# A hybrid attention layer: the cross-attention scores in two PSUM banks of their own, directly behind the stick-breaking scores

## The chip, the cores and the metric

The kernel runs on one core of one Trainium2 chip. The metric is the device time of one execution in microseconds (us). Three runs of the kernel before took 1628.17, 1628.67 and 1628.81 us, so the median is 1628.67 us. A separate execution was profiled; all rows below are from that one.

## The reference, cut to what matters

One layer over 4096 tokens of width 1024. RMSNorm(x) goes through one input projection of width 3072, whose parts feed three branches; each branch is multiplied by silu of its gate, and the three side by side go through an output projection that is added to x.

```
h = rmsnorm(x, norm_g)
sb_q, sb_k, sb_v, sb_gate, lru_x, lru_gate, xa_q, xa_gate = split(h @ w_in)
# stick-breaking attention: 8 heads of 64, q and k normed, strictly causal
z = q @ k.T / 8 ; log_fail = where(s < t, -softplus(z), 0)
w = where(s < t, exp(log_sigmoid(z) + sum of log_fail over the later keys), 0) ; sb = w @ v
# recurrent branch: causal convolution of 4 taps, two gates, a linear scan over time
h_t = a_t * h_(t-1) + u_t
# cross-attention: 4 heads of 64, q and k normed, 256 memory tokens
xa = softmax(xq @ mk.T / 8) @ mv
out = x + concat(sb * silu(sb_gate), lru * silu(lru_gate), xa * silu(xa_gate)) @ w_out
```

## The kernel before, in words

The tokens are worked on in NT = 32 tiles of 128. All weights stay in SBUF as pairs of float16 halves (high and low), and a product is three matmuls per 128 input columns: high by high, high by low, low by high (`pair_product`, L1479 to L1481). `project(c, ...)` is one 512-wide chunk of the input projection, 24 matmuls of 128x512; there are six per tile, in the order q, k, cross-attention q with its gate, recurrent input with its gate, stick-breaking gate, v. They alternate between PSUM banks 0 and 1. The output projection is two more such products (`out_first`, `out_second`).

The order is written out by hand: each engine runs `body(n, p)` for n from -1 to 33 (most of them in a loop over pairs of steps), and semaphores tie the engines together. `have(engine, signal, tile)` makes the engine wait until `signal` has been raised for `tile`. In step n the input projection is that of tile n, the scores and the rest of the attention are those of tile n-1, the output projection is that of tile n-2, and x of tile n+1 is prepared. Each engine and each DMA queue takes its instructions strictly in order.

PSUM has eight banks of 512 float32 columns. Banks 0 and 1 are `PROJ`, 2 and 3 `SCORE` (one for the even heads, one for the odd), 4 and 5 `TURN`, 6 `SMALL`, 7 `HEADS`. In the steady loop nothing uses `TURN`; only the set-up in steps -1 and 0 does (`memory_turn`, `memory_keys_turn`), and a tail that is entered only where the attention has to look further back than the neighbouring keys (`row`).

TensorE's step n, in its order:
- `project(0)` (q).
- `near_scores(1)`: two transposes (L1510) for the convolution, then 48 small matmuls of 64x64 by 128 columns (L1523), the stick-breaking scores of tile n-1, into `SCORE`. They wait until the exponentials of tile n-2 have read `SCORE` (`p_done`).
- `project(1)` (k), `project(2)` (cross-attention q and gate).
- the cross-attention scores of tile n-1: 12 matmuls of 64 rows by 256 columns (L1598), also into `SCORE`. They wait for `sig`, the sigmoids that have read the stick-breaking scores out of it.
- eight float32 matmuls for the recurrent gates (L1609), `project(3)`, `project(4)`, the 48 matmuls that multiply the stick-breaking weights with v (L1641), `project(5)`.
- `spread_rows` (L1620): two matmuls that spread the row scales of tile n+1 over the partitions. They wait for the diagonal that VectorE makes (`x_diag`, L1189).
- `out_first`, `out_second`, `values_product` (L1559 to L1564).

ScalarE's step n: `project(0)`'s result out of PSUM and its squares, the four sigmoids over `SCORE` (L711, L712, raising `sig`), after `project(1)` the keys out of PSUM (L752) and their squares (L754), after `project(2)` xq and its gate (L768 to L771), then the stick-breaking weights to float16 (L719), the recurrent gates (L787 to L794), the four exponentials of the cross-attention over `SCORE` (L801), the squares of x of tile n+1 (L809), the recurrent input and its gate (L814, L815), the float16 halves of q, k and xq (L822), a square root (L832), the gate sigmoid of `project(4)` (L836), the exponentials to float16 (L845), v (L857), x to float16 (L864). Four of these need another table (ACT_TABLE_LOAD).

VectorE's step n: the convolution, the sums of q's squares, those of k's squares (L1140), the stick scan (L1150) and the weights (L1156), the sums for xq, the low halves (L1168), the maximum of the cross-attention scores over `SCORE` (L1229), the norms (L1241), steps for the recurrent gates, the gates' products (L1201), the low halves of q, k, xq (L1261), the recurrent scan (L1276), the diagonal of the row scales (L1189), and what follows for x and the output.

SyncE issues the DMAs. Ahead of the transposing DMAs of q, k and xq of tile n it waits for `xa_scores`, since the xq buffer is read by L1598. At n = 31 (`last_one`) a second `near_scores(0)` follows the last projections but one, and waits for those DMAs.

Of the kernel before, what the change touches and what calls it, by code (L numbers as in the profile page):

```python
# [32 lines left out]
ACT = mybir.ActivationFunctionType  # L33
# [16 lines left out]
def hybrid_layer(nc, x, x_turned, mem, w_in_g, w_out_g, w_kv_v, per_partition, gain_rows, gate_blocks, out):  # L50
# [4 lines left out]
    HD = 64  # L55
    HS = D // 2 // HD
    HX = D // 4 // HD
    NM = mem.shape[1]
# [27 lines left out]
    with ctx:  # L86
# [24 lines left out]
        probs = fail_g[:, at:at + HX * NM].rearrange("p (h m) -> p h m", m=NM)  # L111
# [18 lines left out]
        xq_t = sb("xq_t", [P, 2, HX // 2, P], F16)  # L130
# [3 lines left out]
        mk_t = sb("mk_t", [P, 2, HX // 2, NM], F16)  # L134
# [65 lines left out]
        mx = few(HX)  # L200
# [31 lines left out]
        SCORE = bank[2:4]  # L232
        TURN = bank[4:6]
# [11 lines left out]
        s = {n: sem("t_" + n) for n in names}  # L245
# [3 lines left out]
        qk_turned = sem("qk_turned")  # L249
# [52 lines left out]
        def have(eng, signal, tile, each=1, short=0, ahead_of_loop=False):  # L302


            if not isinstance(tile, int) or tile >= 0:
                eng.wait_ge(signal, each * (tile + 1) - short)
                if ahead_of_loop or (not isinstance(tile, int) and eng.engine.name in alone):
                    eng.sem_inc(passed, 1)
# [332 lines left out]
        def _(act):  # L641
# [58 lines left out]
            def body(n, p):  # L700
# [3 lines left out]
                last_one, after, end = near_end(n)  # L704
# [22 lines left out]
                if B and not after:  # L727
                    have(act, qk_turned, n - 1, 96)
                    for part in range(2):
                        last = act.activation(k_t[:, p, part, :, 0:HALF], k_t[:, q, part, :, P:], ACT.Copy)  # L730
# [47 lines left out]
                if B:  # L778

                    have(act, s["gates_done"], n - 1)  # L780
                    have(act, s["h_done"], n - 2)
                    if isinstance(n, int) and n == 1:
                        act.wait_ge(mv_made, 2)
                    for g, (dst, bias) in enumerate(((rec_g, brg), (in_g, big))):
                        for h in range(LH):
                            at = (g * LH + h) * P
                            last = act.activation(dst[:, h, :], SMALL[:, at:at + P], ACT.Sigmoid, bias=bias[:, h:h + 1])  # L787
                    last.then_inc(s["gates_read"], 1)
                    have(act, s["gates_read"], n - 1)
                    if isinstance(n, int) and n == 1:  # L790
                        act.wait_ge(lam_made, 2)
                    for h in range(LH):
                        act.activation(tanh_l[:, h, :], rec_g[:, h, :], ACT.Tanh, scale=rate[:, h:h + 1])
                        last = act.activation(decay[:, h, :], rec_g[:, h, :], ACT.Exp, scale=rate[:, h:h + 1])  # L794
                    last.then_inc(s["tanh_done"], 1)

                    have(act, s["neg_done"], n - 1)
                    have(act, s["rden_done"], n - 2)
                    have(act, s["p_low"], n - 2)
                    for h in range(HX):  # L800
                        last = act.activation(probs[:, h, :], SCORE[h % 2][:, (h // 2) * NM:(h // 2 + 1) * NM], ACT.Exp,  # L801
                                              bias=neg_mx[:, h:h + 1], scale=near_scale[:, 1:2], accum_out=den[:, h:h + 1])
                    last.then_inc(s["p_done"], 1)
                if X:
# [6 lines left out]
                if A:  # L811
# [8 lines left out]
                    for raw, half in zip((q_raw, k_raw, xq_raw), halves_of_heads(n, 0)):  # L820
                        scale = QTOP if raw is not k_raw else gain_inv[:, 0:1]
                        last = act.activation(half, raw[:, :, :].rearrange("p h d -> p (h d)"), ACT.Copy, scale=scale)  # L822
# [82 lines left out]
        def _(dve):  # L905
# [180 lines left out]
            def body(n, p):  # L1086
# [22 lines left out]
                last_one, after, end = near_end(n)  # L1109
# [116 lines left out]
                if B:  # L1226
                    have(dve, s["xa_scores"], n - 1)
                    for odd in range(2):
                        last = dve.tensor_reduce(mx[:, odd::2], SCORE[odd][:, :].rearrange("p (h s) -> p h s", s=NM),  # L1229
                                                 AX.X, ALU.max)  # L1230
                    last.then_inc(s["mx_done"], 1)
                    have(dve, s["mx_done"], n - 1)
                    dve.tensor_scalar(neg_mx[:, :], mx[:, :], past_scale[:, 1:2], None, ALU.mult).then_inc(s["neg_done"], 1)
# [3 lines left out]
                if A:  # L1237
                    have(dve, s["rs_done"], n)
                    have(dve, s["k_gained"], n)
                    for raw, at, heads in ((q_raw, 0, HS), (k_raw, HS, HS), (xq_raw, 2 * HS, HX)):  # L1240
                        last = dve.tensor_tensor(raw[:, :, :], raw[:, :, :],  # L1241
                                                 rs[:, at:at + heads].unsqueeze(2).to_broadcast([P, heads, HD]), ALU.mult)
# [13 lines left out]
                if A:  # L1256
                    silu(s["lru_read"], s["gate_l"], PROJ[1][:, LW:GC], slice(D // 2, D // 2 + LW), G_LRU)
                    have(dve, s["qk_high"], n)
                    for raw, high, low in zip((q_raw, k_raw, xq_raw), halves_of_heads(n, 0), halves_of_heads(n, 1)):
                        scale = QTOP if raw is not k_raw else gain_inv[:, 0:1]  # L1260
                        last = dve.scalar_tensor_tensor(low, raw[:, :, :].rearrange("p h d -> p (h d)"), scale, high,  # L1261
                                                        ALU.mult, ALU.subtract)
# [10 lines left out]
                if B:  # L1273
                    have(dve, s["u_done"], n - 1)
                    for h in range(LH):
                        last = dve.tensor_tensor_scan(h_sb[:, h, :], decay[:, h, :], in_g[:, h, :],  # L1276
                                                      h_sb[:, h, P - 1:P], ALU.mult, ALU.add)
# [157 lines left out]
        def _(pe):  # L1435
# [3 lines left out]
            def chunk_wide(c):  # L1439

                pe.wait_ge(w_top, c + 1)
                if c:
                    pe.wait_ge(w_factor, c)
                pe.matmul(HEADS[:, 0:P], ones[:, :], w_diag, start=True, stop=True).then_inc(w_wide, 1)
# [40 lines left out]
            def body(n, p):  # L1485
# [15 lines left out]
                last_one, after, end = near_end(n)  # L1501

                def near_scores(d):

                    have(pe, s["lru_read"], n - d)
                    have(pe, s["y_mixed"], n - 2)
                    if d == 0:
                        have(pe, s["gates_read"], n - 1)
                    for c in range(LH):
                        last = pe.transpose(SMALL[:, (2 + c) * P:(3 + c) * P], lx_raw[:, c * P:(c + 1) * P], ident[:, :])  # L1510
                    last.then_inc(s["turned_lx"], 1)
                    if static and n == 1:
                        pe.wait_ge(zeroed, 5)
                    have(pe, qk_turned, n - d, 96)
                    have(pe, s["k_halo"], n - d - 1)
                    have(pe, s["p_done"], n - d - 1, ahead_of_loop=True)
                    keys = k_t[:, (p, q)[d]]
                    for c in range(HS // 2):
                        for a, b in ((0, 0), (0, 1), (1, 0)):
                            for top in (0, HALF):  # L1520
                                for odd in range(2):
                                    r = slice(odd * HD, (odd + 1) * HD)
                                    last = pe.matmul(SCORE[odd][top:top + HALF, c * HW:(c + 1) * HW],  # L1523
                                                     q_t[r, a, c, top:top + HALF], keys[r, b, c, top:top + HW],
                                                     start=a + b == 0, stop=a == 1)
                    last.then_inc(s["scores"], 1)

                def out_first():

# [48 lines left out]
                if B and not after:  # L1578
                    if static and n == 1:
                        pe.wait_ge(m_evac, MT + 1)  # L1580
                    near_scores(1)

                project(1, [(s["v_read"], n - 1), (s["out_ready"], n - 3)])
                if static and n == 0:
# [4 lines left out]
                if static and n == 0:  # L1589
                    memory_product(0, 1)  # L1590
                    chunk_wide(4)
                if B:
                    have(pe, s["sig"], n - 1)
                    for c in range(HX // 2):
                        for a, b in ((0, 0), (0, 1), (1, 0)):
                            for odd in range(2):
                                r = slice(odd * HD, (odd + 1) * HD)
                                last = pe.matmul(SCORE[odd][:, c * NM:(c + 1) * NM], xq_t[r, a, c, :], mk_t[r, b, c, :],  # L1598
                                                 start=a + b == 0, stop=a == 1)
                    last.then_inc(s["xa_scores"], 1)  # L1600
                    have(pe, s["conv"], n - 1, TAPS)
                    if after:
                        have(pe, s["y_mixed"], n - 2)
                    if static and n == 1:
                        pe.wait_ge(blocks_loaded, 16)
                    for g, by_head in enumerate((rg_blocks, ig_blocks)):
                        for h in range(LH):
                            at = (g * LH + h) * P
                            last = pe.matmul(SMALL[:, at:at + P], by_head[:, h, :], xc[:, h, :], start=True, stop=True)  # L1609
                    last.then_inc(s["gates_done"], 1)  # L1610
# [33 lines left out]
                if last_one:  # L1644
                    near_scores(0)
# [108 lines left out]
```

## Time and profile before

| what | value |
|---|---|
| median of three runs | 1628.67 us |
| profiled execution, its own time | 1626.99 us |
| its span, first to last instruction | 1625.3 us |
| TensorE busy | 1540.7 us (95%) |
| VectorE busy | 1072.4 us (66%) |
| ScalarE busy | 878.9 us (54%) |
| GpSimd busy | 309.7 us (19%) |

The profiled execution's time is 1.7 us more than its span. Busy times count a matmul from its start to its modelled end, so that overlapping matmuls look gapless: a 128x512 matmul is listed with 0.38 us though the next one starts 0.22 us later. Where a short stall of TensorE is looked for, the starts of neighbouring matmuls say more than the busy share.

### The profile page before, as it was taken

The numbers are of one execution on the slowest core, as the hardware profiler recorded it, in microseconds if no ns is written. First come the engines' busy times: TensorE is split into PE (matmuls) and PEld (weight loads), VectorE is DVE, ScalarE is ACT, GpSimd is POOL, SyncE is SP. The second block draws the span as 40 slices with busy tenths as digits, with TensorE's granted clock in tenths as the row PEclk, the third lists the DMA queues.
The fourth block names the chain that finished last, engine by engine and source line by source line (L and its number), as shares of the span: only waits on it lengthen the run. The fifth ranks groups of instructions, "written<-read, shape, count | busy, mean of one in ns | idle before, by whom it ended". The sixth has DMA issues, their size and how long they took to land.

```text
span 1625.3 us, 30070 instructions
## 1 busy us (share of the span) xinstructions
PE 1540.7 (95%) x10886; PEld 751.3 (46%) x10886; DVE 1072.4 (66%) x1962; ACT 878.9 (54%) x1581; POOL 309.7 (19%) x278
## 2 busy tenths in 40 slices
PE   3875999999999999999999999999999999999976
PEld 1332444444444444444444444444444444444432
DVE  5876766666667666666766666667666666766662
ACT  5855654445566544555655445566544555665450
POOL 0211221111222221112221212222221112221200
PEclk9887999999999999999999999999999999999987
DMA  9423445455454454544545455454454545445543
GB/s 368 182 57 88 110 118 131 121 118 117 122 126 107 126 136 100 139 105 123 122 117 128 124 115 121 118 126 109 126 133 102 137 107 125 120 115 129 114 79 102
DMA packets 368560, 201.52 MB, mean 124 GB/s; under 512 B 333776, under 2 KB 334224, under 8 KB 367376
## 3 DMA queue, kind: packets, MB, share of 16 engines
q1 hardware_dynamic: 368240, 200.98, 48.3%
q8 instruction: 18, 0.29, 0.1%
q10 hardware_dynamic: 288, 0.13, 0.0%
q14 instruction: 14, 0.11, 0.0%
HBM read 70.73 MB, written 50.53 MB: 75 GB/s over the span
## 4 chain that ended last, share of the span: by engine, by line
PE 71%; ACT 14%; issue 7%; DVE 5%; DMA 1%; POOL 1%; SPq 0%; ACTq 0%; POOLq 0%; DVEq 0%
PE bank L1479 21%; PE bank L1480 21%; PE bank L1481 21%; ACT fail_and_take L801 2%; PE bank L1523 2%; DVE w_pair L1011 1%; ACT spare L822 1%; ACT L815 1%; ACT L794 1%; ACT L836 1%; ACT L832 1%; PE bank L1609 1%; ACT fail_and_take L809 1%; PE bank L1620 1%; PE bank L1641 1%
## 5 line engine op out<-in xcount | busy, mean ns | idle before, releaser
L1479 PE MATMUL bank<-w_pair,x_hi 128*128 128x512 f16 x1536 | 587.7, 383 | 14.4 <-DVE gate L1201 7.2
L1480 PE MATMUL bank<-w_pair,x_hi 128*128 128x512 f16 x1536 | 586.8, 382 | 0.0
L1481 PE MATMUL bank<-w_pair,x_lo 128*128 128x512 f16 x1536 | 585.9, 381 | 0.0
L1479 PEld LDWEIGHTS bank<-w_pair,x_hi 128*128 128x128 f16 x1536 | 151.0, 98 | 192.1 <-issue 10.7
L1481 PEld LDWEIGHTS bank<-w_pair,x_lo 128*128 128x128 f16 x1536 | 151.1, 98 | 184.3 <-issue 5.0
L1480 PEld LDWEIGHTS bank<-w_pair,x_hi 128*128 128x128 f16 x1536 | 151.0, 98 | 167.1 <-issue 3.8
L872 ACT ACTIVATE spare<-xy,columns 128x1024 f16<-128x1024 f32 x32 | 36.7, 1147 | 346.2 <-DVE columns L1351 346.2
L1479 PE MATMUL bank<-wo_pair,y_hi 128*128 128x512 f16 x512 | 196.2, 383 | 9.5 <-DMA y_lo<-spare 9.5
L1480 PE MATMUL bank<-wo_pair,y_hi 128*128 128x512 f16 x512 | 196.2, 383 | 0.0
L1481 PE MATMUL bank<-wo_pair,y_lo 128*128 128x512 f16 x512 | 196.0, 383 | 0.0
L582 POOL TENSOR_TENSOR fail_and_take<-fail_and_take,seen 128x512 f32<-128x512 f32 x32 | 42.4, 1325 | 688.8 <-ACT fail_and_take L712 688.8
L603 POOL TENSOR_TENSOR rs<-rs,columns 128x20 f32<-128x20 f32 x32 | 141.5, 4423 | 5.5 <-POOL rs L601 5.1
L1140 DVE TENSOR_REDUCE ss<-turned 128x8 f32<-128x512 f32 (+1 forms) x96 | 57.0, 593 | 93.5 <-ACT turned L754 90.6
L1174 DVE SCALAR_TENSOR_TENSOR spare<-bank,y_un,spare 128x512 f32<-128x512 f32 x32 | 24.0, 750 | 132.9 <-PE bank L1481 132.9
L1201 DVE SCALAR_TENSOR_TENSOR gate<-bank,unscale,gate 128x256 f32<-128x256 f32 (+1 forms) x96 | 54.5, 568 | 67.1 <-ACT gate L836 63.2
L1150 DVE TENSOR_TENSOR_SCAN fail_and_take<-fail_and_take,restart 128x516 f32<-128x516 f32 x64 | 95.1, 1524 | 4.3 <-POOL fail_and_take L582 4.3
L864 ACT ACTIVATE x_hi<-x_t 128x1024 f16<-128x1024 f32 x32 | 33.8, 1056 | 94.3 <-DVE x_t L1194 94.3
L1479 PEld LDWEIGHTS bank<-wo_pair,y_hi 128*128 128x128 f16 x512 | 50.5, 99 | 67.8 <-DMA y_lo<-spare 10.1
L768 ACT ACTIVATE xq_raw<-bank,unscale 128x256 f32<-128x256 f32 x32 | 15.1, 473 | 122.2 <-PE bank L1481 118.5
L1481 PEld LDWEIGHTS bank<-wo_pair,y_lo 128*128 128x128 f16 x512 | 50.5, 99 | 61.7 <-issue 2.2
L1480 PEld LDWEIGHTS bank<-wo_pair,y_hi 128*128 128x128 f16 x512 | 50.4, 99 | 57.9 <-issue 1.9
L1241 DVE TENSOR_TENSOR q_raw<-q_raw,rs 128x512 f32<-128x512 f32 x32 | 37.6, 1176 | 56.4 <-POOL rs L603 56.4
(233 smaller groups left out, 2415.0 us busy)
## 6 DMA issues: line engine op xcount, KB each, us to landing
xy<-in_x SPq DMA_DIRECT2D x32, 512.0 KB, 3.4
x_t<-in_x_turned SPq DMA_DIRECT2D x32, 512.0 KB, 4.7
spare<-in_x SPq DMA_DIRECT2D x32, 512.0 KB, 4.2
out<-spare SPq DMA_DIRECT2D x32, 512.0 KB, 2.6
wo_pair<-in_w_in SPq DMA_DIRECT2D x4, 2048.0 KB, 12.3
gate_kept<-gate SPq DMA_DIRECT2D x32, 256.0 KB, 2.2
v_kept<-v_sb SPq DMA_DIRECT2D x32, 256.0 KB, 2.1
fail_and_take<-v_sb SPq DMA_DIRECT2D x64, 128.0 KB, 2.3
```

The source lines that it names most:

```text
L582: pool.tensor_tensor(take[:, :, HALF:], take[:, :, HALF:], seen[:, :].unsqueeze(1).to_broadcast([P, HS, HALF]), ALU.mult).then_inc(s["mask ...
L603: pool.tensor_tensor(rs[:, :], rs[:, :], mhalf_c[:, :].to_broadcast([P, 20]), ALU.pow).then_inc(s["rs_done"], 1)
L801: last = act.activation(probs[:, h, :], SCORE[h % 2][:, (h // 2) * NM:(h // 2 + 1) * NM], ACT.Exp, bias=neg_mx[:, h:h + 1], scale=near_sca ...
L864: act.activation(x_hi[:, :, :], x_t32[:, :, :], ACT.Copy).then_inc(s["x_hi_done"], 1)
L872: act.activation(y_halves[:, 0, :], xy[:, :], ACT.Copy, scale=y_top[:, :]).then_inc(s["y_high"], 1)
L1140: dve.tensor_reduce(ss[:, at:at + heads], squares[:, 0:heads * HD].rearrange("p (h d) -> p h d", d=HD), AX.X, ALU.add).then_inc(done, 1)
L1150: last = dve.tensor_tensor_scan(flat, flat, restart[:, ::-1], 1.0, ALU.mult, ALU.max)
L1201: dve.scalar_tensor_tensor(gate[:, p, cols], src, unscale[:, group:group + 1], gate[:, p, cols], ALU.mult, ALU.mult).then_inc(done, 1)
L1241: last = dve.tensor_tensor(raw[:, :, :], raw[:, :, :], rs[:, at:at + heads].unsqueeze(2).to_broadcast([P, heads, HD]), ALU.mult)
L1479: pe.matmul(dst, hi[:, k, :], pair[:, 0, k, :], start=k == 0, stop=False)
L1480: pe.matmul(dst, hi[:, k, :], pair[:, 1, k, :], start=False, stop=False)
L1481: last = pe.matmul(dst, lo[:, k, :], pair[:, 0, k, :], start=False, stop=k == KD - 1)
```

## The change

The cross-attention scores (L1598) move from behind `project(2)` to directly behind the stick-breaking scores, ahead of `project(1)`, and go into banks 4 and 5 (`TURN`). In the step after the last tile (`after`) they stay where they were. Their wait for `sig` is dropped; in its place they wait until the exponentials of the tile before have read `TURN` (`p_done`), and for xq's DMA. The stick-breaking scores now wait for `sig` of the tile before, no longer for `p_done`. ScalarE's exponentials (L801) and VectorE's maximum (L1229) read `TURN`; their places in their queues are as before. The number and form of all instructions but the waits is as before.

```diff
@@ ScalarE
-                        last = act.activation(probs[:, h, :], SCORE[h % 2][:, (h // 2) * NM:(h // 2 + 1) * NM], ACT.Exp,
+                        last = act.activation(probs[:, h, :], TURN[h % 2][:, (h // 2) * NM:(h // 2 + 1) * NM], ACT.Exp,
@@ VectorE
-                        last = dve.tensor_reduce(mx[:, odd::2], SCORE[odd][:, :].rearrange("p (h s) -> p h s", s=NM),
+                        last = dve.tensor_reduce(mx[:, odd::2], TURN[odd][:, :].rearrange("p (h s) -> p h s", s=NM),
@@ TensorE, near_scores
-                    have(pe, s["p_done"], n - d - 1, ahead_of_loop=True)
+                    have(pe, s["sig"], n - d - 1, ahead_of_loop=True)
...
+                def memory_scores(d):
+
+                    have(pe, s["p_done"], n - d - 1)
+                    have(pe, qk_turned, n - d, 96)
+                    for c in range(HX // 2):
+                        for a, b in ((0, 0), (0, 1), (1, 0)):
+                            for odd in range(2):
+                                r = slice(odd * HD, (odd + 1) * HD)
+                                last = pe.matmul(TURN[odd][:, c * NM:(c + 1) * NM], xq_t[r, a, c, :], mk_t[r, b, c, :],
+                                                 start=a + b == 0, stop=a == 1)
+                    last.then_inc(s["xa_scores"], 1)
@@ TensorE, body
                     near_scores(1)
+                    memory_scores(1)
 
                 project(1, [(s["v_read"], n - 1), (s["out_ready"], n - 3)])
...
+                if after:
+                    memory_scores(1)
                 if B:
-                    have(pe, s["sig"], n - 1)
...
-                                last = pe.matmul(SCORE[odd][:, c * NM:(c + 1) * NM], xq_t[r, a, c, :], mk_t[r, b, c, :],
-                                                 start=a + b == 0, stop=a == 1)
-                    last.then_inc(s["xa_scores"], 1)
                     have(pe, s["conv"], n - 1, TAPS)
```

## Rows read from the trace of the kernel before

**Rows 1.** The page: busy us, share and instructions.

```profile
PE 1540.7 (95%) x10886; PEld 751.3 (46%) x10886; DVE 1072.4 (66%) x1962; ACT 878.9 (54%) x1581; POOL 309.7 (19%) x278
```

**Rows 2.** Busy time by stretch: the stretch, us, busy us of each engine, PEclk.

```profile
240.00:1500.00 1260.00, 1259.32 (x9062) 617.38 (x9060) 837.43 (x1481) 683.18 (x1264) 256.04 (x216) 1.00 0.49 121
```

**Rows 3.** Waits of ScalarE, 240 to 1500 us: total us, times, longest.

```profile
ACT xq_raw L768 <- PE bank L1481: 106.7, 27, 4.0
```

**Rows 4.** Waits of TensorE's weight loads, 240 to 1500 us.

```profile
PEld bank L1620 <- DVE spare L1189: 13.6, 27, 0.6
```

**Rows 5.** The chain that ended last, 740 to 760 us: start, us, what.

```profile
740.92 0.47 ACT xq_raw L768
...
756.76 0.70 ACT gate L836
...
758.99 0.19 DVE spare L1189
...
759.23 0.49 PE bank L1620 x2
```

**Rows 6.** TensorE in order of time, step's end, one tile and the next.

```profile
712.00 0.38 PE L1481 MATMUL bank<-w_pair,x_lo 128*128 128x512 f16 x1
712.34 0.49 PE L1620 MATMUL bank<-spare,ones 128*128 128x128 f32 x2
...
758.80 0.38 PE L1481 MATMUL bank<-w_pair,x_lo 128*128 128x512 f16 x1
759.23 0.49 PE L1620 MATMUL bank<-spare,ones 128*128 128x128 f32 x2
```

**Rows 7.** TensorE in order of time around the stick-breaking scores.

```profile
728.95 0.38 PE L1481 MATMUL bank<-w_pair,x_lo 128*128 128x512 f16 x1
729.16 0.38 PE L1510 MATMUL bank<-ident,lx_raw 128*128 128x128 f32 x2
```

**Rows 8.** TensorE in order of time around the cross-attention scores.

```profile
740.42 0.38 PE L1481 MATMUL bank<-w_pair,x_lo 128*128 128x512 f16 x1
740.73 0.83 PE L1598 MATMUL bank<-mk_t,xq_t 64*128 64x256 f16 x12
741.49 1.16 PE L1609 MATMUL bank<-xc,gate_blocks 128*128 128x128 f32 x8
```

**Rows 9.** Lines L1598 and L1620: min/median/max ns, first and last start.

```profile
L1598 PE MATMUL bank<-mk_t,xq_t x384: 268/269/281, 120.1 to 1575.4; 64*128 64x256 f16 x192
...
L1620 PE MATMUL bank<-spare,ones x60: 274/376/583, 154.1 to 1508.8; 128*128 128x128 f32 x60
```

**Rows 10.** ScalarE in order of time: last stick-breaking sigmoid; keys in step 1.

```profile
732.37 0.70 ACT L712 ACTIVATE fail_and_take<-bank,columns 128x512 f32<-128x512 f32 x1
...
115.77 0.69 ACT L752 ACTIVATE k_raw<-bank,unscale 128x512 f32<-128x512 f32 x1 [3.43 <-DVE ss L1140]
```

**Rows 11.** VectorE in order of time: maxima, and the product for the recurrent gate.

```profile
744.36 1.28 DVE L1229 TENSOR_REDUCE columns<-bank 128x2 f32<-128x512 f32 x2
...
752.38 0.48 DVE L1201 SCALAR_TENSOR_TENSOR gate<-bank,unscale,gate 128x256 f32<-128x256 f32 x1
```

**Rows 12.** TensorE: `project(5)`'s first matmul; matmuls behind two early gaps.

```profile
753.82 0.39 PE L1479 MATMUL bank<-w_pair,x_hi 128*128 128x512 f16 x1
...
33.41 0.39 PE L1479 MATMUL bank<-w_pair,x_hi 128*128 128x512 f16 x1 [1.15 <-DVE w_pair L1011]
33.63 0.38 PE L1480 MATMUL bank<-w_pair,x_hi 128*128 128x512 f16 x1
...
142.44 0.61 PE L1479 MATMUL bank<-w_pair,x_hi 128*128 128x512 f16 x1 [7.24 <-DVE gate L1201]
...
145.82 0.46 PE L1481 MATMUL bank<-w_pair,x_lo 128*128 128x512 f16 x1
```

**Rows 13.** Waits of TensorE over the whole span.

```profile
PE bank L1523 <- DMA xq_t<-spare: 7.3, 1, 7.3
...
PE bank L1641 <- DMA turned<-spare: 1.6, 1, 1.6
```

More of the change, by code:

```diff
@@ L1591, in body @@
                     chunk_wide(4)
+                if after:
+                    memory_scores(1)
                 if B:
-                    have(pe, s["sig"], n - 1)
[L1594 to L1597, printed above, removed]
-                                last = pe.matmul(SCORE[odd][:, c * NM:(c + 1) * NM], xq_t[r, a, c, :], mk_t[r, b, c, :],
-                                                 start=a + b == 0, stop=a == 1)
-                    last.then_inc(s["xa_scores"], 1)
                     have(pe, s["conv"], n - 1, TAPS)
```

## The prediction

> **What bounds the kernel now.** I read the busy shares first. TensorE is busy 95% of the span and the other engines 66% or less [rows 1]; between 240 and 1500 us it is busy 1259.32 of 1260.00 us at the full clock [rows 2]. By that alone TensorE would be the bound, and moving twelve of its matmuls within the step would be worth nothing. The busy share hides short stalls here, because a matmul counts as 0.38 us though the next starts 0.22 us later, so I read the waits next. ScalarE stands still for TensorE before it reads `project(2)` out of PSUM (L768), 106.7/27 = 4.0 us in each step [rows 3]. And TensorE's weight load for `spread_rows` (L1620) waits for VectorE's diagonal (L1189) in each of those 27 steps [rows 4].
>
> The chain of waits puts the two together [rows 5]. In this step it runs down TensorE to the last matmul of `project(2)` (740.42 [rows 8]), starts ScalarE's L768 at 740.92, stays on ScalarE until L836 ends at 757.46, crosses to VectorE for the recurrent scan and the diagonal, which ends at 759.18, and returns to TensorE at L1620, 759.23. From L768's start to L1620 that is 759.23 - 740.92 = 18.31 us. Along this stretch the reader should see pieces that follow each other with no other engine's work between: ScalarE's queue has no wait for another engine in it.
>
> How much of that TensorE stands still is in the starts. A float32 matmul behind a 128x512 one starts 729.16 - 728.95 = 0.21 us after it when nothing is missing [rows 7]. L1620 starts 712.34 - 712.00 = 0.34 and, a step later, 759.23 - 758.80 = 0.43 us after [rows 6]. So TensorE stalls only 0.13 and 0.22 us per step, by turns. But it stalls in every step: the period of 759.23 - 712.34 = 46.89 us is the way on TensorE from L1620 to the end of `project(2)` plus the 18.31 us through ScalarE and VectorE. TensorE's work behind `project(2)` runs beside that chain and just falls short of covering it. This is a loop with two nearly equal sides, and it matters on which side of `project(2)` a matmul stands.
>
> **The change part by part.** *The move.* Behind `project(2)` the twelve matmuls lie beside ScalarE's chain; ahead of `project(1)` they delay both reads of ScalarE that it starts from. From the first of them to the next group's first it is 741.49 - 740.73 = 0.76 us [rows 8]. Part of that is a change of matmul form: L1598 itself starts 740.73 - 740.42 = 0.31 us after a 128x512 matmul, where 0.22 is the pitch, so a change costs 0.09. The work alone: the twelve run in pairs, the last starts 0.83 - 0.27 = 0.56 us after the first [rows 8, 9], that is five pitches of 0.11, and a sixth makes 0.67. In the new place there is already a change between the scores and `project(1)`; if the change from 64x64 to 64x128 is free, `project(1)` starts 0.67 us later, if it costs the same 0.09, 0.76, and if each side of the group costs 0.09 more than now, 0.85. I take 0.76, the nearest row.
>
> The Trainium skill, TensorEngine Tiling (Array Packing), section Tiling Modes, states that a change of tiling mode, as against a change of tile, drains TensorE. It lists 64x64 and 64x128 as different modes. By that rule the delay is the 0.76 form; without it, with both groups counted as one mode, 0.67. No row of this trace shows a switch between those two forms.
>
> What does this delay cost? `project(1)` and `project(2)` both end 0.76 us later. VectorE's side (sums of k's squares, scan, weights) starts from L752 and shifts by as much, ScalarE's side starts from L768 likewise, and no link between L768 and L1189 is fed by something that moves less. So the diagonal comes 0.76 us later, while L1620's place in TensorE's queue is even 0.09 earlier, because behind `project(2)` one change of form is gone. The stall at L1620 grows from 0.13 or 0.22 us to about 0.98 or 1.07, and the period by 0.76.
>
> *How many steps.* L1620 has 60 matmuls in 30 steps, first at 154.1 and last at 1508.8 [rows 9]; the first, step 1, is in the set-up. Steps 2 to 30, 29 of them, are in the loop described. In step 31 TensorE waits 7.3 us for xq's transposing DMA [rows 13]; that DMA is fed by ScalarE's halves of q, k and xq behind L768, so this step pays as well: 30 steps. In step 32 the scores stay in place. In step 1 ScalarE's L752 waits for VectorE, not for TensorE, and starts at 115.77 [rows 10]; of the 0.76 between nothing and all comes through, and since another engine is the later one there I take 0.15. Sum: 30 x 0.76 + 0.15 = 22.95, say 23.0 us.
>
> *The waits.* The dropped wait for `sig`: the last sigmoid ends at 732.37 + 0.70 = 733.07 [rows 10] and TensorE reaches the scores at 740.73 [rows 8], 7.7 us later. Nothing stood there, so nothing is gained. The new waits: `sig` of the tile before (733.07 less a period of 46.9) has been there for some 43 us when the stick-breaking scores begin. `p_done` of the tile before comes from L801, which ScalarE does before L836; L836 ends at 757.46 [rows 5], a period earlier at 710.6, and the scores begin behind L1510, at 729.4 [rows 7], 19 us later. xq's DMA is the same one that the stick-breaking scores already wait for. Behind these waits stands all of TensorE's queue, beginning with `project(1)`, but there is no time to lose in them: 0 us, and with the cover gone it would be 1:1.
>
> *The readers.* VectorE's maxima (L1229) do not wait for the scores: they start at 744.36 [rows 11], right when their queue gets to them, and the scores were done at 741.6. Earlier scores bring nothing. The exponentials stand behind other ScalarE work likewise. Reading banks 4 and 5 instead of 2 and 3 changes no duration that a row shows: 0. SyncE's wait for `xa_scores` is satisfied earlier, but its transposes wait for the halves L822, later still: 0.
>
> *What gets close.* `project(5)` waits for VectorE's product of the recurrent gate, which ends at 752.38 + 0.48 = 752.86 [rows 11]; TensorE starts `project(5)` at 753.82 [rows 12], 0.96 us later. Of that the 0.76 leaves 0.2, and the earlier place of TensorE by 0.09 leaves 0.1: still covered, and if it were not, the matmuls delayed would only eat from the stall at L1620. The weights' transposing DMA before L1641 has more room: TensorE waits for it once in the whole span [rows 13].
>
> **The sum.** Profiled execution 1626.99 + 23.0 = 1650.0 us. The median of the runs shown is 1.7 us above that execution, so as a median 1628.67 + 23.0 = 1651.7 us, +1.4%. With 0.67 per step it is 20.2 us more (1648.9), with 0.85 it is 25.7 (1654.4).
>
> **The rivals.** *(A) TensorE's own work sets the period (faster).* If the stall at L1620 were no sign of a tie, or if ScalarE's chain shrank by the 0.85 us needed (from 18.31 to under 17.5) once its exponentials and TensorE's stick-breaking scores no longer share banks, TensorE would run without that stall and with one change of form less: 30 x (0.17 + 0.09) = 7.8 us less, 1620.9. It decides from the point where the diagonal is ready before `project(5)` ends. For it: TensorE's 1259.32 of 1260. Against it: in the steady steps L1620 starts 0.05 us after the diagonal's end (759.18, 759.23), with ScalarE's queue full from L768 on, and nothing in that queue reads `SCORE` at the same time as TensorE writes it. 5%.
>
> *(B) The delay is swallowed (no change).* The move would cost nothing if ScalarE's chain had idle time that a later start squeezes out, as before L752 and L768. It would then be 1628.67 less at most 2.7 (30 x 0.09): 1626 to 1629. Against it: on the chain I see no piece by which ScalarE waits for an engine whose work does not itself start from `project(1)` or `project(2)`. 6%.
>
> *(C) The stall costs TensorE its clock (slower still).* A stall of 1 us per tile is new. After the gap of 7.24 us eight matmuls start in 145.82 - 142.44 = 3.38 us, 0.42 apart, half speed, the 1.2 GHz level; after the gap of 1.15 us they come 0.22 apart, the 2.4 GHz level [rows 12]. If each of 29 stalls brought such a stretch, 29 x 8 x (0.42 - 0.22) = 46 us would be added to the forecast: 1698. The second row speaks against it, and TensorE is otherwise gapless. 4%. By the Trainium skill, TensorE: Matmul & The Clock Gate, section "A second HAM failure mode: psum-queue depth-cycling", short idle spells between groups of matmuls, repeated often enough, make the clock swing between its levels. That is the rule that speaks against this change; the trace shows no case of stalls of this size in every tile, so it stays open by that rule.
>
> **How the numbers follow.** The forecast has 85%, A 5%, B 6%, C 4%. The forecast's own range, from 0.67 to 0.85 per step and a little for the alternation of the stall and step 1, is 1647 to 1656. For 8 in 10 I widen it on the low side, where a part of the delay could be swallowed, to 1642, and to 1658 above. A measurement of this kernel can tell about 0.2% (3.3 us) from no change. Slower by more than that holds the forecast and C, less a little for B's neighbourhood: 0.89; within it 0.06; faster 0.05.
>
> **What would show it right or wrong.** In the changed kernel: the period from L1620 to L1620 about 47.6 us; L1620 starting about 1.0 us or more after the last matmul of `project(5)`, and still 0.05 us after the diagonal's end; from L768's start to L1620 again 18.3 us; `project(1)` starting 0.76 us later behind the stick-breaking scores; ScalarE's waits before L752 and L768 about as long as before or longer, never zero; the granted clock 1.00 from 240 to 1500. The prediction is wrong if the 18.3 us change, if L1620 no longer starts with the diagonal, or if the granted clock falls in the loop.

## Result: 22.3 us slower, by the place of twelve matmuls and not by their banks

Four runs of the changed kernel took 1649.81 to 1652.40 us, median 1650.73; the kernel before, four runs, 1628.42. The ratio is 1.0139, 95% interval 1.0122 to 1.0157: 22.3 us or 1.4% slower. The forecast was 1651.7 us, 23.0 more.

The changed kernel's page has TensorE less busy than [rows 1], in a longer span, with the same number of instructions counted for each engine. (In all there are 30101 where there were 30070; the 31 more are semaphore waits in TensorE's queue.)

```profile
span 1650.6 us, 30101 instructions
...
PE 1538.2 (93%) x10886; PEld 755.3 (46%) x10886; DVE 1072.9 (65%) x1962; ACT 878.0 (53%) x1581; POOL 309.8 (19%) x278
...
PEclk9887999999999999999999999999999999999987
```

Busy time by stretch, changed kernel, in the columns of [rows 2]: 25.5 us of idle TensorE where there was 0.7, and the granted clock still 1.00, the 2.4 GHz level.

```profile
240.00:1500.00 1260.00, 1234.51 (x8953) 610.07 (x8953) 822.41 (x1454) 669.61 (x1233) 249.00 (x211) 1.00 0.48 118
```

TensorE in order of time, changed kernel, around the scores. L1536 is what L1598 was in [rows 8]: `project(1)` now starts 741.90 - 741.14 = 0.76 us after the first of the twelve.

```profile
740.35 0.86 PE L1523 MATMUL bank<-k_t,q_t 64*64 64x128 f16 x48
741.14 0.83 PE L1536 MATMUL bank<-mk_t,xq_t 64*128 64x256 f16 x12
741.90 0.39 PE L1479 MATMUL bank<-w_pair,x_hi 128*128 128x512 f16 x1
```

The same view at the step's end, which answers to [rows 6] (L1627 is `spread_rows`). The stall is long enough now to be listed as a wait.

```profile
721.91 0.38 PE L1481 MATMUL bank<-w_pair,x_lo 128*128 128x512 f16 x1
723.22 0.49 PE L1627 MATMUL bank<-spare,ones 128*128 128x128 f32 x2 [0.93 <-DVE spare L1189]
...
769.52 0.38 PE L1481 MATMUL bank<-w_pair,x_lo 128*128 128x512 f16 x1
770.86 0.49 PE L1627 MATMUL bank<-spare,ones 128*128 128x128 f32 x2 [0.96 <-DVE spare L1189]
771.19 0.38 PE L1479 MATMUL bank<-wo_pair,y_hi 128*128 128x512 f16 x1
```

From the last matmul of `project(5)` to `spread_rows` it is, from start to start, 1.31 and 1.34 us where it was 0.34 and 0.43, and the period (the time of one step) here is 770.86 - 723.22 = 47.64 us (46.89 before). The chain of waits of the changed kernel answers to [rows 5]:

```profile
752.55 0.48 ACT xq_raw L768
...
768.39 0.70 ACT gate L836
...
769.78 0.85 DVE spare L1276 x2
770.63 0.19 DVE spare L1189
...
770.86 0.49 PE bank L1627 x2
```

From L768 to `spread_rows` it is 770.86 - 752.55 = 18.31 us, to the hundredth what it was. So the period grew on TensorE's side of the loop, between `spread_rows` and the end of `project(2)`, and nowhere else. Over all 29 steps of the loop the time from L768's start to the diagonal's end lies within 18.24 and 18.26 us in both kernels, but for the last (18.14 and 18.13).

### The profile page after: what moved, and what is told of

It reads as the page before. It is cut to its first block, busy times and chain, and to the rows that moved or that the text cites. A ratio compares the mean times of both kernels' runs of the same rounds, so it can differ in the third digit from the quotient of the medians.

```text
span 1650.6 us, 30101 instructions
## 1 busy us (share of the span) xinstructions
PE 1538.2 (93%) x10886; PEld 755.3 (46%) x10886; DVE 1072.9 (65%) x1962; ACT 878.0 (53%) x1581; POOL 309.8 (19%) x278
## 4 chain that ended last, share of the span: by engine, by line
PE 56%; ACT 26%; issue 11%; DVE 5%; DMA 1%; POOL 1%; SPq 0%; ACTq 0%; DVEq 0%; POOLq 0%
PE bank L1479 17%; PE bank L1481 16%; PE bank L1480 16%; ACT fail_and_take L801 3%; ACT spare L822 2%; ACT L815 2%; ACT L794 2%; ACT L836 2%; ACT L832 2%; ACT fail_and_take L809 2%; PE bank L1523 2%; DVE spare L1276 1%; PE bank L1536 1%; DVE w_pair L1011 1%; ACT gate L836 1%
## 5 line engine op out<-in xcount | busy, mean ns | idle before, releaser
L768 ACT ACTIVATE xq_raw<-bank,unscale 128x256 f32<-128x256 f32 x32 | 15.2, 474 | 122.2 <-PE bank L1481 118.5
L752 ACT ACTIVATE k_raw<-bank,unscale 128x512 f32<-128x512 f32 x32 | 22.0, 687 | 104.2 <-PE bank L1481 104.2
```

## Experiments

The mean period is taken from the first transpose of step 3 (L1510) to that of step 29, over 26, in each kernel's profiled run. The ratio is to the kernel before, run beside it on the same chip. Its median there was 1628.11 us (beside `banks_alone`, `both_places`, `late_spread_before` and `late_spread_after`), 1628.56 us (beside `between`, `double_ahead`, `diag_first_after` and `late_spread_after_gate_first`) and 1627.81 us (beside `late_spread_before_gate_first`).

```
kernel                         median us   ratio [95%]              mean period us
before                         1628.42     1                        46.847
changed                        1650.73     1.0139 [1.0122, 1.0157]  47.608
banks_alone                    1627.50     0.9996 [0.9987, 1.0005]  46.848
both_places                    1651.25     1.0145 [1.0130, 1.0161]  47.618
between                        1650.72     1.0135 [1.0120, 1.0151]  47.611
double_ahead                   1671.13     1.0263 [1.0249, 1.0277]  48.270
diag_first_after               1628.35     0.9999 [0.9990, 1.0008]  46.859
late_spread_before             1618.91     0.9949 [0.9935, 0.9963]  46.572
late_spread_after              1621.77     0.9961 [0.9947, 0.9974]  46.657
late_spread_before_gate_first  1617.27     0.9937 [0.9923, 0.9950]  46.570
late_spread_after_gate_first   1613.87     0.9909 [0.9894, 0.9925]  46.397
```

**The banks alone** (`banks_alone`).

```diff
                     near_scores(1)
-                    memory_scores(1)
...
-                if after:
-                    memory_scores(1)
                 if B:
+                    memory_scores(1)
```

> The cross-attention scores stay behind project(2), as before, but go into the two TURN banks, with the waits of the change. Theory (the place on TensorE is what costs: everything ahead of project(2) delays ScalarE's chain of 18.3 us): as before, 1628.4, within 1 us. Rival (the banks cost, by the way in which reads and writes share them): the whole rise, 1650.7.

Measured 1627.50 us, period 46.848. So the banks and the new waits, with the matmuls in the old place, change nothing that can be told from the noise. That the new waits cost nothing in the new place either is in the changed kernel's rows above: the twelve start 0.79 us after the first of the 48 scores, and in the kernel before `project(1)`, with no such wait, started 0.80 us after it (rows under "Why the prediction was right"). What is left is the place.

**The same matmuls once more, behind project(2)** (`both_places`).

```diff
+                if B and not after:
+                    have(pe, s["sig"], n - 1)
+                    for c in range(HX // 2):
...
+                                pe.matmul(SCORE[odd][:, c * NM:(c + 1) * NM], xq_t[r, a, c, :], mk_t[r, b, c, :],
+                                          start=a + b == 0, stop=a == 1)
                 if B:
                     have(pe, s["conv"], n - 1, TAPS)
```

> The changed kernel, and in addition the twelve matmuls of the kernel before at their old place, into SCORE, with nobody reading them: 12 matmuls more per step behind project(2). Theory: they cost TensorE 0.85 us per step and fall into its stall of about 1.1 us ahead of spread_rows: no change against the changed kernel, 1650.7, within 1.5 us. Rival (TensorE's amount of work sets the period): 30 x 0.85 = 25 us more, 1676.

Measured 1651.25 us, period 47.618. TensorE does twelve matmuls more in each step and the time does not move. In order of time, `both_places` (L1613 the second set, L1635 `spread_rows`):

```profile
750.51 0.38 PE L1481 MATMUL bank<-w_pair,x_lo 128*128 128x512 f16 x1
750.83 0.83 PE L1613 MATMUL bank<-mk_t,xq_t 64*128 64x256 f16 x12
751.58 1.16 PE L1624 MATMUL bank<-xc,gate_blocks 128*128 128x128 f32 x8
...
768.89 0.38 PE L1481 MATMUL bank<-w_pair,x_lo 128*128 128x512 f16 x1
769.33 0.49 PE L1635 MATMUL bank<-spare,ones 128*128 128x128 f32 x2
```

The distance ahead of `spread_rows` fell from 1.34 to 769.33 - 768.89 = 0.44 us: the second set went into the stall, 0.90 us of it.

**Twice ahead of project(1)** (`double_ahead`).

```diff
-                    for c in range(HX // 2):
+                    for c in [*range(HX // 2)] * (2 if d and not after else 1):
```

> The changed kernel, with its twelve cross-attention matmuls ahead of project(1) issued twice (the second set writes the same values over the first). Theory: 12 matmuls more ahead of project(2), all in one form, so 0.67 us more per step go into the period one to one: 48.28, 31 x 0.67 = 20.5 us more, about 1671. If the switch of form is part of each set: 0.76, about 1674. Rival (the twelve matmuls are not what costs 0.76, but waits or the switch): less than 5 us more.

Measured 1671.13 us, 20.4 more than the changed kernel. TensorE in order of time, `double_ahead`:

```profile
749.87 1.48 PE L1536 MATMUL bank<-mk_t,xq_t 64*128 64x256 f16 x24
751.28 0.39 PE L1479 MATMUL bank<-w_pair,x_hi 128*128 128x512 f16 x1
```

The 24 take 1.41 us where the 12 took 0.76, so the second twelve take 0.65 to 0.66, and the period rose by 48.270 - 47.608 = 0.662. Twelve matmuls more behind `project(2)`, where the stall had room for them, cost nothing; the same twelve ahead of it cost all of their time. What the first group costs beyond that, 0.76 - 0.66 = 0.10 us, is the change of form.

**Between project(1) and project(2)** (`between`).

```diff
                     near_scores(1)
-                    memory_scores(1)
 
                 project(1, [(s["v_read"], n - 1), (s["out_ready"], n - 3)])
+                if B and not after:
+                    memory_scores(1)
```

> The changed kernel, with the cross-attention scores between project(1) and project(2). ScalarE's and VectorE's work behind project(1) is then not delayed, only that behind project(2). Theory (ScalarE's queue from L768 on is the chain, the branch from L752 only runs beside it): L768 is as late as in the changed kernel, plus 0.09 us for a change of matmul form more, period 47.6 to 47.7, about 1651 to 1654. Rival (the branch from project(1) over VectorE's scan and weights sets the chain): period near 46.9, about 1629.

Measured 1650.72 us, just under the range expected; the period, 47.611, is at its low end. The branch from `project(1)` is not what sets the chain. But the price is made up differently: the group itself costs more here. TensorE in order of time, `between`:

```profile
744.89 0.38 PE L1481 MATMUL bank<-w_pair,x_lo 128*128 128x512 f16 x1
745.20 0.83 PE L1536 MATMUL bank<-mk_t,xq_t 64*128 64x256 f16 x12
745.96 0.39 PE L1479 MATMUL bank<-w_pair,x_hi 128*128 128x512 f16 x1
```

It starts 0.31 us behind a 128x512 matmul, a change of form of its own (0.09 over the pitch), and takes 0.76 as well, 0.85 in all, and yet the period is that of the changed kernel. ScalarE in order of time, `between`:

```profile
752.16 0.48 ACT L771 ACTIVATE gate<-bank,unscale 128x256 f32<-128x256 f32 x1
752.51 1.06 ACT L719 ACTIVATE spare<-fail_and_take 128x1024 f16<-128x1024 f32 x1
```

and the same two instructions in the changed kernel:

```profile
753.28 0.48 ACT L771 ACTIVATE gate<-bank,unscale 128x256 f32<-128x256 f32 x1
753.76 1.06 ACT L719 ACTIVATE spare<-fail_and_take 128x1024 f16<-128x1024 f32 x1
```

L719 follows L771 by 0.35 us here and by 0.48 there. In the kernel before it is 0.48 too. L719 waits for VectorE's weights, which come down the branch from `project(1)`. VectorE in order of time, the changed kernel first, then `between`:

```profile
752.43 1.22 DVE L1156 TENSOR_TENSOR fail_and_take<-fail_and_take 128x1024 f32<-128x1024 f32 x1
...
750.44 1.22 DVE L1156 TENSOR_TENSOR fail_and_take<-fail_and_take 128x1024 f32<-128x1024 f32 x1
```

In the changed kernel the weights end at 753.65 and L719 follows 0.11 us later; in `between` they end at 751.66, 0.85 us ahead of L719. With that branch not delayed by the group, a wait of some 0.12 us inside ScalarE's queue goes, and L768 to the diagonal's end falls from 18.25 to 18.15 us. That takes back the 0.09 that the second change of form costs.

**The diagonal ahead of the scans** (`diag_first_after`).

```diff
+                if X and not first:
+                    row_diagonal()
                 if B:
                     have(dve, s["u_done"], n - 1)
...
                     last.then_inc(s["h_done"], 1)
-                if X and not first:
-                    row_diagonal()
```

> The changed kernel, with VectorE's diagonal (L1189) ahead of the recurrent scans (L1276) instead of behind them; TensorE as changed. Theory (the period is TensorE's way to project(2) plus ScalarE's and VectorE's 18.3 us): the scans' 0.77 us leave the chain, which becomes 17.5 us; the period falls from 47.61 to 46.84, the time by 30 x 0.77 = 23 us to about 1628, and the stall ahead of spread_rows from 1.3 to about 0.55 us between starts. Rival (the chain only ends at the diagonal by chance and something else holds TensorE): unchanged, 1650.7.

Measured 1628.35 us, period 46.859. The chain from L768 to the diagonal is 17.50 us, 0.75 shorter, and the period fell by 0.75. The chain of waits of `diag_first_after`, without the scans between L836 and the diagonal:

```profile
712.90 0.70 ACT gate L836
...
714.29 0.29 DVE spare L1189
...
714.62 0.49 PE bank L1627 x2
```

So the other side of the loop is shown too: what is taken off ScalarE's and VectorE's side comes off the period one to one. That the time is that of the kernel before is chance: the scans happen to be as long as the delay of 0.76. TensorE still stalls ahead of `spread_rows` here (0.57 us from start to start on the mean, 0.22 without a wait), so the two sides are not level yet.

**spread_rows later in TensorE's queue** (`late_spread_before`, `late_spread_after`). This takes away what makes TensorE stall: the matmuls that need the diagonal stand behind nine that do not.

```diff
-                    pair_product(PROJ[0][:, :], y_hi, y_lo, wo_pair[:, 0], out_done[0])
+                    if X and A:
+                        pair_product(PROJ[0][:, :], y_hi, y_lo, wo_pair[:, 0], out_done[0], range(3))
+                        spread_rows()
+                        pair_product(PROJ[0][:, :], y_hi, y_lo, wo_pair[:, 0], out_done[0], range(3, KD))
+                    else:
+                        pair_product(PROJ[0][:, :], y_hi, y_lo, wo_pair[:, 0], out_done[0])
...
-                if X and not (static and n == 0):
+                if X and not (static and n == 0) and not C:
                     spread_rows()
```

> The kernel before, with the two matmuls of spread_rows put behind the first nine matmuls of out_first instead of ahead of it. Theory: the stall of 0.13 and 0.22 us per step for VectorE's diagonal goes, TensorE alone sets the period: 30 x 0.17 = 5 us less, about 1623.4, period 46.7. Rival (those stalls are no sign of a tie, TensorE's own work sets the period anyway): 1628.4.

> The changed kernel, with spread_rows behind the first nine matmuls of out_first. Theory: the stall of 0.92 to 0.96 us per step goes. TensorE then arrives at out_first about when VectorE's gate product (L1201, 1.0 us ahead of the diagonal's end) is done, so 0.0 to 0.2 us per step remain: period 46.5 to 46.7, about 1620 to 1625, the whole rise of 22 us gone and a little more. Rival (the rise sits elsewhere, in the waits or the banks): it stays near 1648 to 1650.

Measured 1618.91 and 1621.77 us. The whole rise of the change is gone in the second, and both beat the kernel before; but the order of the change is still the slower of the two. With the kernel before the gain was larger than the 5 us I expected: the period fell by 46.847 - 46.572 = 0.275, not 0.17. TensorE in order of time, `late_spread_after` (L1632 is `spread_rows`):

```profile
711.69 0.38 PE L1481 MATMUL bank<-w_pair,x_lo 128*128 128x512 f16 x1
712.16 0.38 PE L1479 MATMUL bank<-wo_pair,y_hi 128*128 128x512 f16 x1
...
714.10 0.38 PE L1632 MATMUL bank<-spare,ones 128*128 128x128 f32 x2
714.32 0.38 PE L1479 MATMUL bank<-wo_pair,y_hi 128*128 128x512 f16 x1
```

Two things are seen here. Behind the unstalled pair the next matmul starts after 0.22 us, where behind the stalled one it is 771.19 - 770.86 = 0.33: a stalled pair loses another 0.11 us in itself, the share that I had missed. (0.17 of stall on the mean and 0.11 make the 0.275.) And `out_first` starts 0.47 us behind `project(5)`, 0.25 more than the pitch: a new, smaller stall, at the point where the code waits for the gate product of `project(4)`. The next experiment tests that this is the wait.

**The gate sigmoid earlier on ScalarE** (`late_spread_after_gate_first`, and on the order of before `late_spread_before_gate_first`). ScalarE's L836 goes ahead of the square root L832.

```diff
-                if B:
-                    have(act, s["beta_steps"], n - 1, 3)
-                    act.activation(beta[:, :, :], beta[:, :, :], ACT.Sqrt).then_inc(s["beta_done"], 1)
                 if A:
                     have(act, proj_done[4], n)
...
                                    ).then_inc(s["sg_read"], 1)
+                if B:
+                    have(act, s["beta_steps"], n - 1, 3)
+                    act.activation(beta[:, :, :], beta[:, :, :], ACT.Sqrt).then_inc(s["beta_done"], 1)
```

> The changed kernel, with spread_rows behind nine matmuls of out_first, and with ScalarE's gate sigmoid (L836) ahead of the square root (L832). With spread_rows late, TensorE still stalled 0.25 to 0.28 us per step for the gate product ahead of out_first. Theory: that stall goes as well, TensorE alone sets the period, 46.4 to 46.5, and having one change of form less than the order of before with late spread_rows (46.57, 1618.9 us) it is 2 to 5 us faster: 1614 to 1617. Rival (a new wait takes its place, the square root being later by 0.7 us): no better than 1621.8.

> The kernel before (cross-attention scores behind project(2), in SCORE), with spread_rows behind nine matmuls of out_first and ScalarE's gate sigmoid (L836) ahead of the square root (L832). Theory (TensorE alone sets the period once spread_rows is late; the advantage of 0.17 us per step of the same two edits on the changed kernel is its saved change of matmul form): as without the sigmoid's move, period 46.57, about 1619. Rival (the sigmoid's move itself is worth it, whatever the place of the scores): period 46.4, about 1614.

Measured 1613.87 us on the changed kernel's order, just under the range expected. It beats both kernels: 0.9909 of before, interval 0.9894 to 0.9925. On the order of before the sigmoid's move left the period at 46.570, so there TensorE had been the bound already (1617.27 us; its interval overlaps that of `late_spread_before`). The move takes more out of ScalarE's way than the square root itself. ScalarE in order of time, `late_spread_after`, then `late_spread_after_gate_first` (L833 is the gate sigmoid there):

```profile
707.09 0.40 ACT L822 ACTIVATE spare<-xq_raw 128x256 f16<-128x256 f32 x1
...
710.54 0.69 ACT L836 ACTIVATE gate<-bank,unscale 128x512 f32<-128x512 f32 x1
...
702.60 0.41 ACT L822 ACTIVATE spare<-xq_raw 128x256 f16<-128x256 f32 x1
702.91 0.68 ACT L833 ACTIVATE gate<-bank,unscale 128x512 f32<-128x512 f32 x1
```

The sigmoid starts 0.31 us behind the halves of xq where it was 3.45: the square root and the two table loads (1.28 us each) that stood around it are no longer ahead of the sigmoid. The number of table loads is the same in both, 128; one now stands ahead of the first stick-breaking sigmoid (L711). The diagonal gains less, 17.68 us behind L768 where it was 18.26, since the scans now wait for GpSimd (L616); what `out_first` needs is the gate product, and that comes with the sigmoid.

TensorE in `late_spread_after_gate_first` is listed as busy throughout:

```profile
240.00:1500.00 1260.00, 1260.00 (x9162) 628.45 (x9161) 848.47 (x1496) 691.45 (x1274) 262.64 (x219) 1.00 0.49 121
```

By the starts, the stall ahead of `out_first` is gone (0.22 us behind `project(5)`). What is left is 0.05 us ahead of `project(5)` in every second step: 0.18 us from the last of the 48 matmuls of weights by v (L1653) to `project(5)`, where it is 0.13 in the other steps.

```profile
707.20 0.38 PE L1481 MATMUL bank<-w_pair,x_lo 128*128 128x512 f16 x1
707.42 0.38 PE L1479 MATMUL bank<-wo_pair,y_hi 128*128 128x512 f16 x1
...
748.47 0.20 PE L1653 MATMUL bank<-v_sb,turned 128*64 128x64 f16 x1
748.65 0.39 PE L1479 MATMUL bank<-w_pair,x_hi 128*128 128x512 f16 x1
```

With both edits the change's order is thus worth 46.570 - 46.397 = 0.17 us per step, and only now has its idea the sign that was meant. The changed kernel's gates in order of time:

```profile
752.06 0.38 PE L1481 MATMUL bank<-w_pair,x_lo 128*128 128x512 f16 x1
752.27 1.05 PE L1616 MATMUL bank<-xc,gate_blocks 128*128 128x128 f32 x8
753.16 0.38 PE L1479 MATMUL bank<-w_pair,x_hi 128*128 128x512 f16 x1
```

From `project(2)`'s last matmul over the gates to `project(3)` it is now 1.10 us. In the kernel before, that stretch with the twelve in it was 742.49 - 740.42 = 2.07 us, by [rows 8] and this row of the kernel before that follows them:

```profile
742.49 0.38 PE L1479 MATMUL bank<-w_pair,x_hi 128*128 128x512 f16 x1
```

The difference of 0.97 is more than the 0.76 that the twelve take in the new place: the change saves 0.21 us of TensorE, since the change of form ahead of the twelve is gone (0.09) and the gates themselves take 0.89 instead of 1.00 us. The period shows 0.17 of it; most of the rest goes into the small stall ahead of `project(5)`, which `late_spread_before_gate_first` does not have.

## Why the prediction was right

*What bounds the kernel.* Right, and shown from three sides: work ahead of `project(2)` costs its full time (`double_ahead`), work behind it nothing (`both_places`), and time taken off ScalarE's and VectorE's chain comes back one to one (`diag_first_after`).

*The delay, 0.76 us.* Right: 0.76 from start to start, and a period 47.608 - 46.847 = 0.761 longer. The two ends that I kept, 0.67 with a free change of form and 0.85 with two more, are both out. By the Trainium skill (TensorEngine Tiling (Array Packing), Tiling Modes: a change of mode drains TensorE) 0.76 and not 0.67 was expected, and the trace agrees: the twelve start 741.14 - 740.35 = 0.79 us after the first of the 48 scores, and in the kernel before `project(1)`, whose form differs as well, started 0.80 us after it. The last of the 48, which takes 0.22 us, starts 0.86 - 0.22 = 0.64 us after the first. So the next form starts some 0.15 us behind it, where the twelve rounds of four within the 48 come 0.06 apart (0.64 over 11): a change costs 0.09 here too.

```profile
729.47 0.86 PE L1523 MATMUL bank<-k_t,q_t 64*64 64x128 f16 x48
730.27 0.39 PE L1479 MATMUL bank<-w_pair,x_hi 128*128 128x512 f16 x1
```

The length of one of the 48, from the changed kernel's view of that line:

```profile
L1523 PE MATMUL bank<-k_t,q_t x1536: 216/216/312, 110.3 to 1583.5; 64*64 64x128 f16 x192
```

*The steps.* 30 steps of 0.761 are 22.8 us, the medians differ by 22.3. That step 31 pays as well is in the traces: from its transposes to the matmuls that wait for xq's DMA it is 33.15 us, in the kernel before 32.38. The two profiled executions differ by more, 25.3 us of span, of which the set-up has a part: step 2's scores begin 1.7 us later there. Over all kernels run that beginning scatters from 166.4 to 169.5 us, by 2 us and more among kernels of either order, so it is mostly no effect of the change, and no run shows the 0.15 us that I took for step 1.

*The dropped wait, the new ones, the readers, the banks at nothing.* Right together (`banks_alone`, and the start of the twelve above).

*The clock.* The granted clock stayed at 1.00 from 240 to 1500 us, with a stall of 1.1 us in every step. Rival C is out. By the rule on short idle spells (the Trainium skill, TensorE: Matmul & The Clock Gate, "A second HAM failure mode: psum-queue depth-cycling") it could have swung between its levels; this trace, at 1.00 throughout, shows nothing of it.

*Sizes that were off without moving the sum.* I wrote that the place of `spread_rows` would be 0.09 us earlier in TensorE's queue and the distance ahead of it 1.19 and 1.28 us. It is 1.31 and 1.34, 0.94 more than before on the mean, so the place was 0.18 earlier: the gates' shorter run, which I had not counted, less a new small stall ahead of `project(5)`. And rival A priced the stall of the kernel before at 0.17 us per step, where `late_spread_before` showed 0.275. The start distances of single neighbours, from which both were priced, do not see what a group of matmuls loses in itself, 0.10 to 0.11 us both in the eight gates and in the stalled pair.

*Rival A's condition.* I wrote that 0.85 us off ScalarE's chain would let TensorE run without the stall. That does not follow from my own sum, by which the stall grows to 0.98 or 1.07; it measured 1.09 and 1.12 (1.31 and 1.34 less 0.22). `diag_first_after` took 0.75 off and left 0.35 of it.

*What gets close.* I left 0.1 us of cover ahead of `project(5)`. There is none. VectorE and TensorE in order of time, changed kernel (L1648 is the last of the 48 matmuls of weights by v):

```profile
764.01 0.48 DVE L1201 SCALAR_TENSOR_TENSOR gate<-bank,unscale,gate 128x256 f32<-128x256 f32 x1
...
764.37 0.20 PE L1648 MATMUL bank<-v_sb,turned 128*64 128x64 f16 x1
764.55 0.39 PE L1479 MATMUL bank<-w_pair,x_hi 128*128 128x512 f16 x1
```

The gate product ends at 764.49 and `project(5)` starts 0.06 us later, 0.18 behind L1648. In the kernel before the product had been done for 0.96 us [rows 11, 12], and the distance to L1648's counterpart was 0.13. In every second step that is a stall of 0.05 us. As I wrote for this case, it only eats from the stall ahead of `spread_rows`; it comes into the period where that stall is gone (`late_spread_after_gate_first`).

*"No link is fed by something that moves less".* Right for the changed kernel, but my reading that ScalarE's queue has no wait in it was not quite so: `between` shows 0.12 us of wait for VectorE ahead of L719, on the branch from `project(1)`. Since both branches moved by the same 0.76, it did not show.

## What to carry to other kernels

Where TensorE is listed as 99.9% busy, look at the starts of its matmuls around each wait: here a stall of 0.1 to 0.2 us in every step was the place where the loop is closed over two other engines. In such a loop the work ahead of the point from which those engines start cost its whole time, and the same work behind it was free as long as it fitted beside them. Before moving work, ask what the next waiter is. Here moving the waiting matmuls nine places down the queue was worth 9.2 us on the kernel before (1628.11 to 1618.91), more than any place of the scores, and the change's order paid only once the gate sigmoid was moved as well (1613.87 us against 1617.27 with the same two edits on the order of before).

## What the runs showed of the hardware

Two float32 128x128 matmuls that stall at their start for another engine take 0.33 us to the next matmul, in every step of the loop of every kernel with `spread_rows` in its old place; unstalled ones take 0.22 (the four `late_spread` kernels). Eight of them behind the 64x256 matmuls take 1.00 us (kernel before), behind a 128x512 matmul 0.89 (changed kernel). A change of matmul form costs about 0.09 to 0.10 us of TensorE: 0.31 us where 0.22 is the pitch, and 0.76 us for the first twelve matmuls where 0.65 to 0.66 is enough for twelve more in the same form. Between the 64x64 and the 64x128 form it costs as much as between 64x64 and 128x128 (0.79 and 0.80 us from the first of the 48 scores).
